# Moving five modulation parts of a two-block network behind the sums of squares of five norms

## The reference, cut to what matters

```python
mod = cond @ w_ada + b_ada                       # layer 2; layers 0 and 1 the same with mod_w[i], mod_b[i]
shift_m, scale_m, gate_m, shift_f, scale_f, gate_f = split(mod, 6)      # parts 0 to 5
h = rms_norm(x, g_pre_mix) * (1 + scale_m) + shift_m                    # parts 0 and 1
x = x + gate_m * rms_norm(mixer(h), g_post_mix)                         # part 2
h = rms_norm(x, g_pre_ffn) * (1 + scale_f) + shift_f                    # parts 3 and 4
x = x + gate_f * rms_norm(moe_ffn(h), g_post_ffn)                       # part 5
```

## Time and profile before

| | |
|---|---|
| time, median of 3 runs | 2632.06 us (2631.81 to 2633.8) |
| the profiled execution | 2640.1 us, its span 2638.3 us |
| PE busy | 93% of the span |
| PEld / DVE / ACT busy | 48% / 20% / 14% |
| mean granted TensorE clock | 0.955 of full speed |
| moved by DMA | 602.83 MB, mean 228 GB/s |

### The profile page before, as it was taken

One profiled execution on the slowest core, in us unless ns is written; L12 is line 12 of the kernel. 1 busy time (PEld: TensorE's weight loads), 2 busy tenths in 40 slices (PEclk: granted clock), 3 DMA queues, 4 the chain that ended last, 5 costly groups with the idle time before them and its releaser, 6 DMA issues.

```text
span 2638.3 us, 27307 instructions
## 1 busy us (share of the span) xinstructions
PE 2451.0 (93%) x10720; PEld 1268.2 (48%) x10721; DVE 531.5 (20%) x1262; ACT 377.4 (14%) x790; POOL 0.2 (0%) x4
## 2 busy tenths in 40 slices
PE   5999899999999968999996789999999999999997
PEld 2454444444444556888884573333333333333333
DVE  0113312111100123211004332221212212212212
ACT  2212212001100221211114220000000000000001
POOL 0000000000000000000000000000000000000000
PEclk8989999999999988999997588999999999999999
DMA  9536621222222239444441017999988897999895
GB/s 377 211 140 237 212 72 61 72 80 72 72 80 80 96 118 350 159 143 144 146 157 64 1 64 303 417 417 418 418 347 351 332 417 293 418 417 418 343 417 206
DMA packets 212034, 602.83 MB, mean 228 GB/s; under 512 B 10370, under 2 KB 127618, under 8 KB 178946
## 3 DMA queue, kind: packets, MB, share of 16 engines
q1 hardware_dynamic: 209600, 599.04, 59.2%
q10 hardware_dynamic: 2370, 2.88, 0.3%
HBM read 600.83 MB, written 1.05 MB: 228 GB/s over the span
## 4 chain that ended last, share of the span: by engine, by line
PE 84%; DMA 4%; DVE 4%; SPq 3%; ACT 3%; issue 1%; DVEq 0%; ACTq 0%
PE bank L288 52%; PE bank L705 30%; DMA wring<-in_w_gu 4%; SPq L1616 3%; ACT big L837 1%; PE bank L730 1%; DVE big L1175 1%; ACT tmp L837 1%; DVE big L1169 1%; DMA wring<-in_mod_w 1%; ACT hT L837 0%; DVE tmp L1169 0%; DVE tmp L1175 0%; PE bank L584 0%; DVE xT L1175 0%
## 5 line engine op out<-in xcount | busy, mean ns | idle before, releaser
L705 PE MATMUL bank<-wring,big 128*64 128x512 f32 x3456 | 768.7, 595 | 18.7 <-DMA wring<-in_w_gu 9.7
L288 PE MATMUL bank<-hT,wring 128*128 128x256 f32 (+1 forms) x2240 | 725.6, 486 | 14.8 <-ACT hT L837 14.8
L288 PEld LDWEIGHTS bank<-hT,wring 128*128 128x128 f32 x2240 | 427.2, 192 | 311.5 <-issue 268.5
L705 PEld LDWEIGHTS bank<-wring,big 128*64 128x64 f32 x3456 | 240.3, 137 | 493.5 <-issue 444.3
L288 PE MATMUL bank<-big,wring 128*128 128x256 f32 (+1 forms) x1096 | 344.6, 477 | 8.0 <-DVE big L1169 4.0
L288 PEld LDWEIGHTS bank<-big,wring 128*128 128x128 f32 x1096 | 210.0, 192 | 142.0 <-issue 115.9
L837 ACT ACTIVATE big<-bank 128x256 f32<-128x256 f32 (+3 forms) x241 | 108.9, 452 | 912.0 <-PE bank L730 521.3
L1172 DVE TENSOR_SCALAR big<-bank 128x512 f32<-128x512 f32 (+1 forms) x73 | 50.0, 685 | 486.7 <-PE bank L705 486.7
L705 PE MATMUL bank<-big 64*128 64x256 f32 (+1 forms) x872 | 142.1, 465 | 2.8 <-DVE big L1172 2.4
L705 PEld LDWEIGHTS bank<-big 64*128 64x128 f32 (+1 forms) x872 | 74.7, 171 | 79.5 <-issue 73.8
L288 PE MATMUL bank<-wring,cs 128*32 128x256 f32 x1152 | 73.6, 413 | 35.5 <-ACT cs L837 25.4
(11 more groups left out here) (128 smaller groups left out, 1028.2 us busy)
## 6 DMA issues: line engine op xcount, KB each, us to landing
wring<-in_w_gu SPq DMA_DIRECT2D x256, 1024.0 KB, 15.4
wring<-in_w_down SPq DMA_DIRECT2D x128, 1024.0 KB, 14.7
wring<-in_mod_w SPq DMA_DIRECT2D x48, 1024.0 KB, 11.1
wring<-in_ffn_w_up SPq DMA_DIRECT2D x44, 1024.0 KB, 5.2
wring<-in_w_ada SPq DMA_DIRECT2D x24, 1024.0 KB, 6.9
wring<-in_ffn_w_down SPq DMA_DIRECT2D x16, 1024.0 KB, 5.1
wring<-in_w_in SPq DMA_DIRECT2D x14, 1024.0 KB, 5.0
wring<-in_ev_w_in SPq DMA_DIRECT2D x12, 1024.0 KB, 10.6
```

The costliest lines, as they stand in the source:

```text
L288: ins = pe.matmul(o, l, r, start=start, stop=stop, skip_group_check=True)
L705: ins = pe.matmul(o, l, r, start=start, stop=stop, skip_group_check=True)
```

## The change

Five of the twelve parts of layers 1 and 2 move. `IN_NORM` says which part stands in which norm: part 5 of layer 1 (from attention unit 13) in norm 1, parts 0, 3 and 4 of layer 2 (from the retention) in norms 2, 3 and 4. On PE the matmuls stand directly behind the norm's sum of squares, and `turn_rows` behind the first projections that follow; on ACT `take_rows` stands behind the norm's last chunk; on DVE the modulation stands some steps later. Part 5 of layer 2 stands behind the sum `"post"`: its `take_rows` ahead of ACT's squares for norm 5, its `turn_rows` behind the router's matmuls, its DVE step ahead of the gates. Parts 1 and 2 of layer 2 stay in the retention, at h = 1 and 2.

```diff
-        MOD_U = (2, 4, 6, 8, 11, 13)
+        MOD_U = (2, 4, 6, 8, 11)
+        IN_NORM = {1: (1, 5), 2: (2, 0), 3: (2, 3), 4: (2, 4)}
+        MOD_ORDER = [(m, part) for m in range(3) for part in range(6)]
...
@@ PE @@
                      lambda c: pe.wait_ge(G("x_squared"), DC * n + c + 1))
+                if n in IN_NORM:
+                    modulation(*IN_NORM[n])
...
                     project([("fb", l, 2 * jj + i) for i in range(2)], colsrc(ffn_w_up[l], FFN + 256 * jj), n, T)
+                    if jj == 0:
+                        turn_rows(*IN_NORM[n])
...
             project([("rk", 0), ("rk", 1)], colsrc(win, 768), 2, T2)
+            turn_rows(*IN_NORM[2])
...
-                modulation(2, h)
-                if h:
+                if h in (1, 2):
+                    modulation(2, h)
+                if h in (2, 3):
                     turn_rows(2, h - 1)
                 if h:
                     ret_out(h - 1)
-            modulation(2, 5)
-            turn_rows(2, 4)
-            turn_rows(2, 5)
...
                 project([("frg", 2 * i), ("frg", 2 * i + 1)], colsrc(win, 2048 + 256 * i), 4, S)
+                if i == 0:
+                    turn_rows(*IN_NORM[4])
...
             stat("post", ones, [hT[:, c, 0:S] for c in range(DC)], lambda c: freed(pe, ("wo2", c)))
+            modulation(2, 5)
             norm(5)
...
+            turn_rows(2, 5)
             for tt in range(2):
                 for g in range(2):
                     bk, fl = claim(("h2", tt, g), 6)
@@ ACT @@
                     ins.then_inc(G("h_ready"), 1)
+                if n in IN_NORM:
+                    take_rows(*IN_NORM[n])
...
-                if part >= 2:
-                    full(act, ("mod", m, part - 2))
+                i = MOD_ORDER.index((m, part))
+                if i >= 2:
+                    full(act, ("mod", *MOD_ORDER[i - 2]))
...
-            take_rows(2, 0)
...
-                take_rows(2, h + 1)
+                if h < 2:
+                    take_rows(2, h + 1)
...
-            take_rows(2, 5)
             logs()
...
             rstd("post", tmp[:, 0, 0:S], D, S).then_inc(G("post_rstd"), 1)
+            take_rows(2, 5)
             norm(5, lambda c: act.wait_ge(G("x_mixed"), c + 1))
@@ DVE @@
+                    if j == 1:
+                        modulation(*IN_NORM[1 + 2 * l])
                 residual(("dn", l), l, 5, T)
...
             ins.then_inc(G("dist"), 1)
+            modulation(*IN_NORM[2])
...
-                if u % 2 and u > 1:
+                if u in (5, 7):
                     modulation(2, u // 2 - 1)
-            for part in range(3, 6):
-                modulation(2, part)
...
                 TS(KD[h], KE[h], sm[:, 36 + h:37 + h], sm[:, 32 + h:33 + h], MUL, ADD).then_inc(G("forget"), 1)
+                if h == 1:
+                    modulation(*IN_NORM[4])
...
                 TS(sm[:, 122:123], sm[:, 32:33], 1.0, None, MUL).then_inc(G("neg_top"), 1)
+            modulation(2, 5)
             for tt in range(2):
                 dve.wait_ge(G("gate_exp"), tt + 1)
```

## The result

The median of four runs is 2613.94 us (2608.24 to 2615.01); the kernel before has 2632.79 us, with one run more than stood ahead of the prediction. The ratio is 0.9924, 95% interval 0.9907 to 0.9941: 18.9 us by the medians, 15.5 to 24.5 us by the interval. Timed once more, the same kernel gave 2613.28 us and 0.9926 (0.9913 to 0.994), 20.1 us by the medians.

The account below looks back on a forecast made before the run. PE, busy 93% of the span, was taken to bound the kernel. Terms -19.0 - 2.4 + 0.7 + 1.6 + 1.1 + 0.55 - 0.5 = -18.0 us off the median 2632.06 gave 2614.0 us, range 2606 to 2620.

Parts of the forecast that it names:

- The retention, -19.0 us: Ahead of `wo1`: DVE's pooling begins sooner and keeps its 13.90 us to `wo1`, so `wo1` starts 19.0 us sooner.
- the dip: At the start of `wo1`: the lower granted clock costs 2.4 us, and it stays because PE idles ahead as before.
- ACT's `rstd` would be just in time: Retention heads: ACT's `rstd` until about 1013.3, DVE wants the first at about 1014.5; cover thin by 1.2 us but enough.
- The attention, -2.4 and +0.7: Unit 14: DVE's maxima start 2.4 us sooner; a lower clock takes back 0.7 us, between -1.6 and +2.3.
- The norms, +1.6 and +1.1: Norms 1 and 2 cost 0, norms 3 and 4 +0.8 us each; four uncovered `turn_rows` cost 1.1 us.
- Behind "post": After the sum "post": ACT catches up after `take_rows`, costing 0; `turn_rows` at the lower clock costs +0.55 us.
- the -0.5 for a later fall of the clock: Behind the sum "post": with the part in the pause the clock may fall later; -0.5 us, between 0 and -6.
- only PE's work: Rival: pooling is held by something unseen, the retention gives 15.5 us, the attention gives back 2.4: 2620 us; chance 0.15.
- late weights: Rival: weights of parts in norms not on chip, 9 us at each of five places, +45: 2659 us; chance 0.03.
- the part does not fit: Rival: at its places the part runs at the lower clock, 3 us more at each of five: 2629 us; chance 0.03.
- The better clock: Rival: behind "post" higher clock lasts through router and transposes, some 6 us, perhaps 2.4 in `wo1`: 2606 us; chance 0.12.

Follow-up runs that it names:

- the reordered pooling: Kernel before, only DVE's order changed: pooling groups 0 and 1 ahead of the modulation of part 3, groups 2 and 3 ahead of parts 4 and 5; 2623.66 us, 0.9965.
- the early pooling: Changed kernel with DVE's pooling moved up between the multiplications of the retention's scores 3 and 4; 2604.14 us, 0.9886 of the kernel before.
- the first experiment: Kernel before with only part 5 of layer 1 moved, from attention unit 13 to norm 1; 2634.83 us, 1.0004.
- both old-code experiments: Kernel before with only part 5 of layer 1 moved to norm 1 (2634.83 us), and with only DVE's pooling order changed (2623.66 us).
- one later kernel: Kernel with early pooling, layer 1 parts in units 2, 5, 8, 11, 14, and layer 2 parts 1 to 4 ahead of the retention's first scores; 2589.12 us, 0.9839.

## Why the prediction was right

It said 2614.0 us, in 2606 to 2620; 2613.94 was measured. The mechanism was right where the gain is, in the retention. That the total agrees to 0.1 us is luck: the interval of the gain is 9 us wide, and two terms were off in opposite directions.

- **The retention, -19.0 us: right.** The first pair of traces has 17.6 to `wo1`, and 1.5 us of the rest is the clock in the first projections, which rose later in this execution (16.70 us where it was 15.24). Over two profiles of the old code and five of the changed the mean difference is 18.7 us to `wo1` and 19.2 to norm 3's sum. `wo1` kept its dip (30.09 us); at full clock it takes 28.00, so the dip is worth 2.1 us, not 2.4. The mechanism is shown by the reordered pooling alone, and by the early pooling after the change. That ACT's `rstd` would be just in time held too: its last one ends at 1009.84, the products begin at 1010.86, a cover of 1.0 us where 1.2 was predicted.
- **The attention, -2.4 and +0.7: the 2.4 was right, the 0.7 mis-sized.** There are five profiles with neither unit 13 nor unit 14 holding a part; PE pauses for 3.9 us in all five and the clock falls in all five. In four the stretch takes 28.60 or 28.61 us: the clock took 2.25 us, at the bad end of the range I gave it (2.3), and 0.15 us is gained, not 1.7. In the fifth, the changed kernel's second profile, it took 0.6 and 1.8 us is gained. On the mean of the profiles, from unit 13's projection to norm 1's sum, the gain is 0.6 us.
- **The norms, +1.6 and +1.1: the steps were right, the base was wrong.** I wrote that norm 4's pause is norm 3's again and that in all four the clock stays up, and had shown it behind norm 1 only. In norm 4 of the kernel before it did not:

```profile
1307.00:1311.00 4.00, 3.22 (x9) 2.53 (x10) 2.29 (x7) 3.97 (x8) 0.00 (x0) 0.68 0.01 2
```

  The twelve profiles show how it is. With a part in the pause of norms 1 to 4, in 29 cases, the clock stays at 1.00 in the 16 us behind it. With the pause empty, in 19 cases, it falls in ten: in 1 of 5 behind norm 1, 3 of 4 behind norm 2, 2 of 5 behind norm 3 and 4 of 5 behind norm 4.

  The stretches follow. (The kernel with the parts behind the first projections is left out here: its stretches hold the parts uncovered.) From norm 3's sum to norm 4's it takes 235.38 us in each of seven with the part in the pause; in four without it, 234.22, 234.23, 235.52 and 235.61. From norm 2's sum to the first scores it takes 84.67 to 84.69 us in eight with the part; in three without, 84.46, 85.40 and 85.40. From norm 1's sum to norm 2's, 464.78 or 464.79 us with the part; without, 464.57 three times and 465.44 once.

  Against an undisturbed pause the part costs what I said (235.38 - 234.22 = 1.2 us in norm 3, 1.1 predicted with its `turn_rows`), but behind an empty pause the longer time, 0.9 to 1.4 us more, comes in five of the eleven cases. On the mean of these cases norm 1 costs 0, norm 2 -0.4 and norm 3 +0.5 us. Norm 4's stretch holds other pauses of PE and varies more (237.9 to 239.8 us with the part, 238.2 to 239.7 without), so its part's cost can't be told; the means of the changed and the old code differ by -0.3. Together that is about nothing instead of 2.7 us.
- **Behind "post": right.** `take_rows` delays only squares that can wait; `turn_rows` costs 0.49 us (0.55 predicted). Of the -0.5 for a later fall of the clock nothing is to be seen in the time. The fall did come later: 6 to 8 us behind the start of the sum the clock was 0.50 in the kernel before and is 1.00 now. But the router's matmuls start 15.5 us behind it in all twelve profiles and run at 0.50 as before, and "post" to the end takes 1092.4 and 1092.9 us in the changed kernel and 1092.4 in the first experiment.

So an attention too good by about 1.1 us stood against norms too dear by about 2.9. The mean stretches sum to some 20 us, the terms to 18.0, and the medians of the two timings give 18.9 and 20.1.

The rule of the Trainium skill ("TensorE: Matmul & The Clock Gate", section "Why this matters for your kernels"), that idle gaps between bursts send the clock back, I had set aside for norms 1 to 4 on the strength of norm 1's row. The page names only longer gaps than the 2.3 us of norms 3 and 4, to which the prediction stretched it. The runs bear it out in part: behind the empty 3.4 us of norms 1 and 2 the clock fell in 4 of 9 cases, behind the 3.9 us in unit 14 in five profiles of five, and behind the 2.3 us of norms 3 and 4 in 6 of 10. Behind pauses that a part fills, the stretches from norms 1, 2 and 3 repeat to 0.02 us.

The rivals: "only PE's work" is ruled out by the reordered pooling, "late weights" by PE's waits (none for a `mod_w` or `w_ada` slot in any norm), and "the part does not fit" by 3.66 us in each norm. The better clock was real in the norms; behind "post" it did not last to the router and gave no time. Why a pause of one length drops the clock in one execution and not in the next stays open.

## What to carry to other kernels

Follow the last releaser ahead of a stage, not the work that is taken out: here one in-order engine (DVE) had 10 us of ready work queued behind bookkeeping for a later stage, and moving that order alone gave 9.5 of the 19 us. Independent filler belongs in the longest waits of the bounding engine first (two parts in a wait of 22.9 us cost nothing at all, and four, which filled it to 1.86 us, gave back 3.4 us of clock behind it), then in short ones, and last beside a projection, where nothing hides its 3.6 us. Taking filler out of a place can cost what it saves, if the engine then pauses and loses its clock: read the granted clock in every pause, in more than one execution.

## What the runs showed of the hardware

An empty pause of PE of 2.3 us (norm 3) was followed by a loss of 1.3 to 1.4 us in two profiles out of four and by none in the other two; in one of the two losses the granted clock stands at 0.70 in the 3.1 us behind the pause. With the pause filled, the same place repeats to 0.01 us in seven profiles. Behind a pause of 1.72 us (unit 15, with the part in unit 14) the clock fell in one profile of four. Behind the retention's long wait (22.9 us, or 15.9) the first projections took 15.24 to 16.70 us in eleven profiles, and 14.08 in the twelfth, where parts filled the wait. How long a fall lasts is not fixed either: 2.25 or 0.6 us lost behind the same pause of unit 14. And one profiled execution of the old kernel took 301.3 us up to the first changed instruction, where the others take 295 to 298, and 1096.9 us behind the last, where both old-code experiments take 1092.4 and 1092.5 (one later kernel took 1095.0): the difference of the two spans alone would have read 25 us where the medians give 19.
